# A two-layer hybrid backbone on one core: RWKV inverse reordered, and weight residuals on GpSimd cut into four instructions

## What is computed

```
def update(S, w_t, k_t, v_t, a_t, b_t):              # state S: 64 x 64, per head, per token, two directions
    sa = jnp.einsum('bhvk,bhk->bhv', S, a_t)
    return S * w_t[:, :, None, :] + sa[..., None] * b_t[:, :, None, :] + v_t[..., None] * k_t[:, :, None, :]
y = einsum(S, r_t)
yl = concatenate([att_l, rw_l]) @ w_out              # then x = x + gate * rms_norm(yl), MLP: square(relu(h @ w1)) @ w2
```

## Time and profile before

| what | us |
|---|---|
| median of 3 runs | 2335.82 (2312.77 to 2336.96) |
| the profiled execution | 2336.36 |
| its span, first to last instruction | 2334.5 |
| PE busy in it | 2099.0 (90%) |
| mean granted TensorE clock | 0.893 |

### The profile page before, as it was taken

The page is one execution under the profiler, slowest core; times in us unless marked ns, Lnnn a source line. Parts: engine busy times, 40 slices in busy tenths (PEclk is TensorE's granted clock), DMA queues, the critical chain, the costliest instruction groups (busy, mean ns, idle before and its releaser), DMA issues. The chain is left out here.

```text
span 2334.5 us, 37122 instructions
## 1 busy us (share of the span) xinstructions
PE 2099.0 (90%) x15738; PEld 1564.3 (67%) x15738; DVE 882.8 (38%) x1372; ACT 572.9 (25%) x818; POOL 874.5 (37%) x340
## 2 busy tenths in 40 slices
PE   7799799799699879969997799999989988999996
PEld 2588467476376647637665488888758764888884
DVE  0312466633443253344326621121350746121125
ACT  2323345310221021022103233233132213232230
POOL 0523001392166039216605334444344324443442
PEclk9899899896698589669858899999989998999998
DMA  6311000031023003102302122232212221223221
GB/s 231 120 54 60 12 1 0 10 134 41 1 74 110 1 10 133 42 1 74 110 5 72 36 86 95 90 108 90 72 54 90 72 72 51 94 91 108 90 98 46
DMA packets 23309, 159.95 MB, mean 69 GB/s; under 512 B 2576, under 2 KB 3216, under 8 KB 4624
## 3 DMA queue, kind: packets, MB, share of 16 engines
q1 hardware_dynamic: 21600, 151.86, 18.4%
q10 hardware_dynamic: 1584, 6.19, 0.7%
HBM read 155.94 MB, written 2.10 MB: 68 GB/s over the span
## 5 line engine op out<-in xcount | busy, mean ns | idle before, releaser
L206 POOL TENSOR_TENSOR v<-raw,v 128x2048 fp32r<-128x2048 f32 x80 | 373.9, 4674 | 558.3 <-ACT v L195 469.8
L222 PE MATMUL bank<-hm,v 128*128 128x512 f32 x2304 | 541.2, 397 | 18.9 <-DVE hm L1615 10.0
L222 PEld LDWEIGHTS bank<-hm,v 128*128 128x128 f32 x2304 | 439.6, 192 | 121.2 <-issue 16.6
L175 PE MATMUL bank<-cst 128*128 128x512 f32 (+2 forms) x920 | 415.4, 564 | 33.3 <-ACT Pn L855 23.8
L222 PE MATMUL bank<-hid,v 128*128 128x512 f32 x1536 | 349.5, 389 | 0.0
L222 PEld LDWEIGHTS bank<-hid,v 128*128 128x128 f32 x1536 | 288.2, 188 | 60.0
L175 PEld LDWEIGHTS bank<-cst 128*128 128x128 f32 x920 | 177.4, 225 | 145.4 <-issue 96.0
L195 ACT ACTIVATE v<-raw 128x2048 fp32r<-128x2048 f32 x73 | 139.9, 1916 | 418.8 <-PE bank L222 418.8
L1242 POOL TENSOR_TENSOR raw<-raw,cs 128x2048 f32<-128x2048 f32 x40 | 144.3, 3609 | 141.1 <-PE bank L1034 141.1
L222 PE MATMUL bank<-h,w 128*128 128x512 f32 x888 | 166.0, 350 | 14.2 <-POOL w L206 11.3
L222 PEld LDWEIGHTS bank<-h,w 128*128 128x128 f32 x888 | 141.4, 190 | 39.2 <-issue 13.5
(11 more groups left out here) (276 smaller groups left out, 2497.7 us busy)
## 6 DMA issues: line engine op xcount, KB each, us to landing
raw<-w_in SPq DMA_DIRECT2D x143, 1024.0 KB, 4.8
xres<-x_in ACTq DMA_DIRECT2D x1, 2048.0 KB, 8.9
out_T<-xres ACTq DMA_DIRECT2D x8, 256.0 KB, 2.0
kkT<-ctx_in ACTq DMA_DIRECT2D x1, 1024.0 KB, 13.4
csa<-csa_in SPq DMA_DIRECT2D x1, 960.0 KB, 4.7
cst<-cst_in ACTq DMA_DIRECT2D x1, 928.0 KB, 17.0
lw<-lw_in SPq DMA_DIRECT2D x4, 128.0 KB, 4.5
g<-g_in SPq DMA_DIRECT2D x1, 256.0 KB, 2.6
```

Source lines behind the costliest of these rows:

```text
L175: nc.tensor.matmul(out[:, 0:width], K("ones"), cst[:, 0:width], start=True, stop=True)
L206: nc.gpsimd.tensor_tensor(W[1][n % 2][:], raw[n % 2][:], W[0][n % 2][:].bitcast(F32), SUB)\
L222: last = nc.tensor.matmul(bank(b(s, m), 0, hi - lo), W[w][s][:, k, m * P:(m + 1) * P], H[h][:, k, lo:hi], start=(k == 0 and w == h == 0), ...
```

## The change

Two things are changed.

- `pool_lo` issues four instructions, each for two of the eight 256-column rows of the block (128 x 512), instead of one of 128 x 2048. Only the last raises split_ready.
- In the inverse the second product of a level is computed as X * W1 in the layout of X, with XT as the loaded weights and its operands so placed that consecutive products alternate between the halves of rows (out at `[half(h)]` instead of `[half(c)]`). DVE adds it to X in place. The next level's first product so reads X straight away. The transposed copy XT, which only the second product needs, is made from X by `next_xt` behind the first product of the next level (PE transposes into bank 6 or 7, ACT copies), and once more for all three batches behind the last level. The ACT copies are now 15 in a turn instead of 12. All 30 fillers of 192 columns between the products of the inverse are gone.

```
-        nc.gpsimd.tensor_tensor(W[1][n % 2][:], raw[n % 2][:], W[0][n % 2][:].bitcast(F32), SUB)\
-            .then_inc(split_ready[n % 2], 1)
+        for k in range(0, KT, 2):
+            i = nc.gpsimd.tensor_tensor(W[1][n % 2][:, k:k + 2], raw[n % 2][:, k:k + 2],
+                                        W[0][n % 2][:, k:k + 2].bitcast(F32), SUB)
+        i.then_inc(split_ready[n % 2], 1)
...
-                    def next_x(lv, b):
-                        pe.wait_ge(xt_ready, NBT * lv + b + 1)
-                        transposes(XT, b, bank(2 * b + 1)).then_inc(tr_done, 1)
+                    def next_xt(lv, b):
+
+                        t = NBT * lv + b
+                        pe.wait_ge(x_ready, t + 1)
+                        if t >= 2:
+                            pe.wait_ge(xt_ready, t - 1)
+                        transposes(X, b, bank(6 + t % 2)).then_inc(tr_done, 1)
...
                             last.then_inc(w_done, 1)
-                            keep_warm(1, bank(6), WARM)
+                            if lv:
+                                next_xt(lv - 1, b)
                         for b in range(NBT):
                             pe.wait_ge(w_ready, NBT * lv + b + 1)
+                            if lv:
+                                pe.wait_ge(xt_ready, NBT * (lv - 1) + b + 1)
                             for g, h, c in units(b):
-                                k = 2 * g + h
-                                last = nc.tensor.matmul(bank(2 * b, (k - 8 * b) * Q, (k - 8 * b + 1) * Q)[half(c)],
-                                                        W1[half(c), k, :], XT[half(c), k, :], start=True, stop=True)
+                                k, at = 2 * g + h, (g - 4 * b) * Q
+                                last = nc.tensor.matmul(bank(2 * b + c, at, at + Q)[half(h)], XT[half(c), k, :],
+                                                        W1[half(c), k, :], start=True, stop=True)
                             last.then_inc(xx_done, 1)
-                            keep_warm(1, bank(6), WARM)
-                            if b and lv < LVL - 1:
-                                next_x(lv, b - 1)
-                        if lv < LVL - 1:
-                            next_x(lv, NBT - 1)
+                    for b in range(NBT):
+                        next_xt(LVL - 1, b)
...
                     for b in range(NBT):
-                        pe.wait_ge(xt_ready, NBT * (LVL - 1) + b + 1)
+                        pe.wait_ge(xt_ready, NBT * LVL if b == 0 else NBT * (LVL - 1) + b + 1)
...
-                            nc.vector.tensor_tensor(XT[:, k, :], XT[:, k, :], cols(2 * b, b), ADD)\
-                                .then_inc(xt_ready, 1)
+                            xx = psum[b][:, :].rearrange("p (c w) -> p c w", c=2)[:, :, 0:4 * Q]\
+                                .rearrange("p c (g j) -> p c g j", j=Q)
+                            xb = by_head(X, 8 * b, 8 * b + 8)
+                            nc.vector.tensor_tensor(xb, xb, xx, ADD).then_inc(x_ready, 1)
```

More of the change, by code:

```diff
@@ L1218, in _ @@
                     first_xt(NBT - 1)
-                    for lv in range(LVL - 1):
+                    for lv in range(LVL):
                         for b in range(NBT):
-                            act.wait_ge(tr_done, NBT * lv + b + 1)
-                            nc.scalar.activation(X[:, 8 * b:8 * b + 8, :], cols(2 * b + 1, b), ACT.Copy)\
-                                .then_inc(x_ready, 1)
+                            t = NBT * lv + b
+                            act.wait_ge(tr_done, t + 1)
+                            act.wait_ge(xx_done, t + 1)
+                            nc.scalar.activation(XT[:, 8 * b:8 * b + 8, :], cols(6 + t % 2, b), ACT.Copy)\
+                                .then_inc(xt_ready, 1)
                     for b in range(NBT):
@@ L1292, in _ @@
                         for b in range(NBT):
-                            k = slice(8 * b, 8 * b + 8)
-                            if lv == 0:
-                                dve.wait_ge(xt0_ready, b + 1)
                             dve.wait_ge(xx_done, NBT * lv + b + 1)
-                            nc.vector.tensor_tensor(XT[:, k, :], XT[:, k, :], cols(2 * b, b), ADD)\
-                                .then_inc(xt_ready, 1)
+                            xx = psum[b][:, :].rearrange("p (c w) -> p c w", c=2)[:, :, 0:4 * Q]\
+                                .rearrange("p c (g j) -> p c g j", j=Q)
+                            xb = by_head(X, 8 * b, 8 * b + 8)
+                            nc.vector.tensor_tensor(xb, xb, xx, ADD).then_inc(x_ready, 1)
                     for b in range(NBT):
```

## The result

| | runs | median, us | lowest to highest |
|---|---|---|---|
| before | 5 | 2336.8 | 2312.8 to 2337.2 |
| after | 5 | 2269.0 | 2264.2 to 2284.4 |

The ratio is 0.974, 95% interval 0.968 to 0.980. The profiled execution of the changed kernel is the slowest of its five: 2284.4 us, span 2282.6, mean granted clock 0.892 (the two shortest: 0.900). Its span is 51.9 us shorter than the 2334.5 of before; the other 15 us to the median go with a higher mean clock, to which the last experiments come. Single executions of these kernels differ, as far as their mean clocks tell, by the number of scans in which the clock stays high, and the text tells where that matters.

A forecast was written before the change was run, and what follows sets the result against it. PE, busy 2099 of 2334.5 us, was taken to bound the inverse by its own issue. From 2336.4 us, 28 for four RWKV turns and 12.6 for the residuals came off, giving 2296 us, range 2262 to 2322.

The forecast's parts named there:

- Step 1: The inverse by itself: cheaper second products, no fillers, levels of 5.8 us against 9.60; 16 us saved per turn.
- PE still bounds it: In the new inverse, data is ready in time and DVE needs 4.2 us of a level's 5.8, so PE sets the pace.
- The bound below, 10 us: The inverse's lower saving per turn, if every semaphore wait cost a 0.2 us gap and a level took 7.2 us.
- Step 2: The earlier scan meets POOL's modulation work, so 7.4 of 16 us arrive; 7 us per turn taken, 28 in four turns.
- a scan step has two L1315, so it costs two POOL instructions: In the scan, DVE and POOL alternate one instruction each, so each step waits for two POOL instructions or their remainder.
- Step 3: Quartered weight residuals let DVE in after a quarter, in three norms and around projections: 12.6 us in all, bounds 0 to 16.
- the 0.4 us that I took off each norm for the second residual: In three norms, the second residual ends 0.4 us later, cutting the gain from 3.0 to 2.6 us each.
- Rival C: DVE does not get in between back-to-back residual quarters, so the residual change gains nothing: 2308 us, chance 0.14.
- a small gain: At the input projection's start and before the output projection, later residual and earlier DVE chain leave about 1.3 us together.
- B: The inverse's gain arrives whole because L1315 finds room between POOL's instructions: 2260 us, chance 0.12.
- D: Each wait costs PE a gap, the scan starts at 523.3, and quartered residuals bring nothing: 2321 us, chance 0.12.
- E: Without fillers the inverse's clock could fall from 1.00 to 0.50, costing 8 to 36 us per turn: 2412 us, chance 0.12.

The follow-up runs named there:

- the last experiments: On the changed kernel: modulation instructions in quarters (2234.8 us) or eighths (2203.9), small loads (2259.9), fillers back (2279.3), eighths with fillers (2207.3).
- experiments 2 and 3: Old and new inverse, both with quartered residual: modulation work cut to 16 of 256 columns (2217.9, 2172.4 us), or its last two slices held back (2292.2, 2242.1).
- inv_only: The changed kernel with each weight residual again one POOL instruction, so the new inverse alone: 2294.0 us.
- mod_held: The changed kernel with POOL's last two modulation slices of a turn held until the scan's last step, everything computed: 2242.1 us, ratio 0.962 to before.
- held_old: The kernel before with quartered residual and the last two modulation slices held until the scan's last step: 2292.2 us, ratio 0.983 to before.
- mod_quarters: The changed kernel with POOL's modulation product in four instructions and its first addition in two: 2234.8 us; the two executions at 2215 give ratio 0.950 to before.

## Why the prediction was right, and where it wasn't

The forecast, 2296 us, is 12 us above the profiled execution that it was reckoned against and 27 above the median of that session; 15 of the 27 go with the clock, for which it had no term.

**Step 1** gave 12.2 us a turn, not 16. The prices of the instructions were good or a little high (1.22 for 1.31, 1.63 for 1.86 us; the tail from the last second product to the next stage took 5.7 us, 1.2 of it a pause, forecast 4.8). What failed is "PE still bounds it", 5.8 us a level: a term is missing that the sum did not have, 4.2 to 5.3 us a turn of pauses at PE's issue, which end when instructions have come. The bound below, 10 us, was reached by supposing a gap at each wait; that it held the value is luck. The row that could have warned was the earlier trace rows itself: before, PE issued 217 matmuls in 9.6 us; I forecast about 200 in 5.8 us and did not ask whether instructions arrive at that rate.

**Step 2** was right in kind and too dark in size. The modulation work does meet the scan, and by experiments 2 and 3 it alone takes the difference between 12.2 and 8.1 us a turn. I had said that 7.4 of 16 would arrive, a loss of 8.6 us; it was 4.1. The step that failed is "a scan step has two L1315, so it costs two POOL instructions": the pair ran as one (4.09, 0.86, 3.20, 0.72 us), and one of two fell where POOL changed instructions. In turn one 2.8 us of the scan's 3.9 are PE's longer waits, and 1.1 the clock that fell sooner. So the sizes of steps 1 and 2 were both off by 4 us, in opposite directions, and that 7 us a turn came so close to 8.1 is luck.

**Step 3** was right, and a little low: 14.5 us where I had 11.3 for norms and the convolution's projection. The hold ends after one quarter (4.59 to 1.29 us, 3.3 us in each norm), and the 0.4 us that I took off each norm for the second residual did not appear. Rival C had said that DVE does not get in between back-to-back quarters; the 1.29 us of L1592 beside four quarters of 5.02 us refuse it. Before layer 0's output projection I had a small gain, and there the quarters lost 0.8 us; the 2.9 us gained beside it are mostly products at a higher clock, which inv_only, with its whole residuals, has too.

**The rivals.** B (all of the inverse's gain arrives) is what happens if the modulation work is held back, as in mod_held against held_old; in the changed kernel it isn't so. D has the changed kernel's 12 us of the inverse nearly right, and falls with step 3. E (the clock) had its sign, a clock below 1.00 in the inverse, in two turns out of four, but for one stretch of 3.4 us, at a price under 2 us each where it had 8 to 36. The Trainium skill, TensorE: Matmul & The Clock Gate, Part 4 (PE-mode transpose), by which transposes do not count as activity for the clock, was weighed there. With 60 transposes in place of 48 among fewer other columns the new inverse kept 1.00 in turns one and three throughout, and where the clock did fall PE had been standing still (busy for 1.25 of 3.44 us), so the fall doesn't need the rule; most of the inverse's products are no transposes, so it doesn't test it either. The row that speaks against it is still the rise at 438.74.

**What I overlooked** is that the clock of the scan was open. The earlier trace rows show it, 0.50 for 49 us, and I read it as a fact of the stage ("as the clock stands in the scan even with fillers there"). It fell behind one wait of 1.75 us, and without POOL's work there it never fell. The changed kernel shares this with the kernel before, so the forecast did not suffer; the worth of it, 23 us for each scan, is twice what the inverse brought.

## What to carry over

A speed-up that moves a stage forward under another engine's work must be costed at that meeting, with the other engine's single instruction as the unit; and cutting those instructions to a quarter or an eighth was worth more (46 and 77 us between the medians of 2281, 2235 and 2204) than the 16 us of the gain that the meeting cost, though most of that came by the clock. Where a stage runs at the lower clock with PE apparently busy all the time, look at its first few microseconds for one wait of PE before taking the clock as given: here removing it gave 23 us on a stage of 53. Fillers are to be costed with the clock that they hold as well as with the gap that they fill: the same thirty cost 6.2 us a turn up to the scan and were neutral in the median of both kernels.

## What the runs showed of the hardware

- **Instruction fetch can bound PE.** With 64x64 products and no fillers PE stopped inside its groups for 0.4 to 2.3 us, 4.2 to 5.3 us in 38.4, and each pause of 0.3 us and more ended 1.3 to 1.6 us after an instruction packet of 16 KB had landed; with the 1 MB loads the pauses were about twice as long in all as without (18.8 against 9.9 us in four turns). The Trainium skill, Runtime: NRT & Kernel Launch, section "Instruction fetch mechanics", has the fetch hidden by the time that issuing takes; in this stage it wasn't.
- **The same scan runs at either clock.** Its 433 matmuls take 30.3 us at 1.00 when PE waits for nothing and 51 to 57 us at a mean of 0.52 to 0.57, and once the clock is down it mostly stays down to the end of the scan, though PE's records show no gap; in mod_quarters' turn three it came back after 13 us, and the scan took 38.2 us.
- **DVE gets in at POOL's instruction boundaries.** Held times were 4.59, 4.09 and 3.20 us beside instructions of 3.6 to 4.6 us, 1.29 us beside quarters of 1.25 us, as the Trainium skill, SBUF — State Buffer, section "Who interferes with whom", has it with its exclusive lock; a pair of short DVE instructions passed at one boundary together. The quarters cost POOL 14% more time in all (1.335 x 4 against 4.674 us).
